# A two-block model in one program: row scales behind the matmuls, norms from PSUM per token tile, and the first loads on the weights' queue

## The chip, the cores and the metric

The kernel runs on one core of a Trainium2 chip. The metric is the time of one execution on the device in microseconds; the table below gives three runs. Everything is float32. TensorE (PE) multiplies, VectorE (DVE) and ScalarE (ACT) work on tiles of 128 partitions, GpSimd (POOL) and SyncE (SP) mostly issue DMAs.

## The reference, cut to what matters

The input x has 256 tokens of width 1024. A first block of two layers runs over it; each layer is FFN, mixer, FFN, with a norm ahead of and behind each:

```python
def rms_norm(x, g):
    return x * rsqrt(mean(x * x) + 1e-6) * g

for l in range(2):
    h = (silu(n(x, pre1) @ w_gate) * (n(x, pre1) @ w_up)) @ w_down      # width 2816
    x = x + 0.5 * rms_norm(h, post1)
    z = rms_norm(x, mix_pre) @ w_in                                     # 2840 columns
    # attention of three kinds on 1304 columns (with rope), a short convolution on the rest
    h = concat(rms_norm(attn, g_o), rms_norm(conv, g_u)) @ w_out
    x = x + rms_norm(h, mix_post)
    h = (silu(n(x, pre2) @ w_gate) * (n(x, pre2) @ w_up)) @ w_down
    x = x + 0.5 * rms_norm(h, post2)
```

A second block follows: modulation vectors, norms of a context and of x, a projection with a convolution and a state-space scan, a Fourier branch, a sum back into x, a norm, a router, 32 experts of which each token takes four, and a last norm.

## The kernel before, in words

All 256 tokens are worked on at once, as two token tiles of 128 (`m` = 0, 1). The weights come from memory in the order of use as chunks of 128 x 4096 floats (2 MB): SP loads them into a ring of three slots (`sp_stream`, L317). Products of the first block are made of three fp32r matmuls (`matmul3`, L376: hi x hi, hi x lo, lo x hi), so every chunk is cut into two halves, and each half is split: ACT writes the rounded part (`act_split`, L335), DVE the rest (`dve_split`, L347). There are two buffers for split halves. ACT may write one once PE is done with the half two before it. PE takes halves in order: `pe_wide` (L381) multiplies all k-tiles of a 512-column chunk for both token tiles, `pe_deep` (L398) the 1024-column chunks of a down-projection, k-tile by k-tile, with all four PSUM banks open. In both, PE writes banks 0 to 3.

Every engine has its own program, written out by hand in the order of `build` (L2133): each method `pe_...`, `act_...`, `dve_...`, `pool_...` appends to one engine, and semaphores (`up` and `at`) tie them together. An engine works strictly in that order. Two halves of the next stage's weights are always split ahead, so the last two splits of a stage's ACT and DVE programs belong to the next stage, and they stand ahead of the norm that ends the stage.

A norm ahead of a stage (`act_rstd` L419, `dve_rstd` L430): ACT squares both tiles with an accumulator, DVE scales and takes the reciprocal, ACT the square root. Then DVE scales tile 0 and ACT tile 1 by it into `xs` (L438, L444), PE transposes `xs` (`pe_turn`, L452), ACT writes the hi part with the gain as a column scale (L466), DVE the lo part (L480), and PE starts when all of it is there. The norm behind a stage (`act_add_normed` L498, `dve_add_normed` L507): ACT and DVE copy the four banks to `hout`, ACT squares, the root follows as above, and DVE, tile by tile, scales, multiplies by the gain row and adds to x. The same `rstd` helpers serve the merged norm in the mixer (L932, L934), the norms of the context and x, of y, of h2 and of the end in the second block.

In an FFN (L544 to L631) the gate and up chunks of one index `i` follow each other, Silu and product are made by ACT (L594) and DVE (L625), and the hidden part is transposed and split again. PE's gate of `i` waits for the Silu of `i-1`, which stands behind four splits on ACT.

At the start (`begin`, L2117) POOL issues the loads of constants, x, column constants, positions and the gain row, while SP already streams weights. DVE and ACT then make the rope tables, and only then split the first two halves.

Of the kernel before, what the change touches and what calls it, by code (L numbers as in the profile page):

```python
# [60 lines left out]
    "router_act": "top_exp WT",  # L61
}.items() for name in names.split()}
# [174 lines left out]
class Kernel:  # L237
# [79 lines left out]
    def sp_stream(self):  # L317
        sp, at, up = self.nc.sync, self.s.at, self.s.up
        for ch in self.chunks:
            if ch.c >= RING:  # L320
                sp.wait_ge(*self.freed_at(ch.c - RING))
            sp.dma_start(self.ring[ch.slot][:, 0:ch.kt * ch.width], ch.src).then_inc(*up(f"dma_ring{ch.slot}", ch.c))
# [12 lines left out]
    def act_split(self, n=1):  # L335

        act, at, up = self.nc.scalar, self.s.at, self.s.up
        for half in self.halves[self.act_half:self.act_half + n]:
            if half.j == 0:
                act.wait_ge(*at(f"dma_ring{half.chunk.slot}", half.chunk.c))  # L340
# [40 lines left out]
    def pe_wide(self, actT, banks, freed):  # L381
# [16 lines left out]
    def pe_deep(self, actT, kt, part_ready):  # L398
# [3 lines left out]
        while k0 < kt:  # L402
            half, w = self.pe_take()
            for k in range(half.k):
                if part_ready(k0 + k):
                    pe.wait_ge(*at(*part_ready(k0 + k)))
                for m in range(MT):
                    for h in range(2):
                        mm = self.matmul3(self.bank[2 * m + h][:, :], actT,
                                          (slice(None), k0 + k, slice(m * P, (m + 1) * P)),  # L410
                                          w, (slice(None), k, slice(h * 512, (h + 1) * 512)),
                                          k0 + k == 0, k0 + k == kt - 1)
            k0 += half.k
            mm.then_inc(*up("half_used", half.h))
# [15 lines left out]
    def dve_rstd(self, st, width, col):  # L430
        dve, at, up = self.nc.vector, self.s.at, self.s.up
        s = self.stat[:, col:col + MT]
        dve.wait_ge(*at("sum_sq", st, MT - 1))
        dve.tensor_scalar(s, s, 1.0 / width, EPS, ALU.mult, ALU.add).then_inc(*up("mean_sq", st))
        dve.wait_ge(*at("mean_sq", st))
        dve.reciprocal(s, s).then_inc(*up("inv_ms", st))
# [61 lines left out]
    def act_add_normed(self, st, done):  # L498
        act, at, up = self.nc.scalar, self.s.at, self.s.up
        act.wait_ge(*at(*done))  # L500
        for m in range(MT):
            act.copy(self.hout[:, m, 512:D], self.bank[2 * m + 1][:, :]).then_inc(*up("hout_right", st, m))
        act.wait_ge(*at("hout_left", st, MT - 1))
        act.wait_ge(*at("hout_right", st, MT - 1))
        self.act_rstd((st, "post"), self.hout, D, 0)

    def dve_add_normed(self, st, done, scale):  # L507
        dve, at, up = self.nc.vector, self.s.at, self.s.up
        h, s = self.hout, self.stat
        dve.wait_ge(*at(*done))  # L510
        for m in range(MT):
            dve.tensor_copy(h[:, m, 0:512], self.bank[2 * m][:, :]).then_inc(*up("hout_left", st, m))
        self.dve_rstd((st, "post"), D, 0)
        dve.wait_ge(*at("rstd", (st, "post")))
        dve.wait_ge(*at("dma_row", st))
        for m in range(MT):
            dve.tensor_scalar(h[:, m, :], h[:, m, :], s[:, m:m + 1], scale, ALU.mult,
                              ALU.mult).then_inc(*up("hout_scaled", st, m))
            dve.wait_ge(*at("hout_scaled", st, m))
            dve.tensor_tensor(h[:, m, :], h[:, m, :], self.row[:, :], ALU.mult).then_inc(*up("hout_gained", st, m))  # L520
            dve.wait_ge(*at("hout_gained", st, m))
            dve.tensor_tensor(self.x[:, m, :], self.x[:, m, :], h[:, m, :], ALU.add).then_inc(*up("x_new", st, m))
# [3 lines left out]
    def ffn_views(self):  # L526
        self.squares = view(self.work, 0, D)
        self.xs = view(self.work, 1024, MT, D)
# [10 lines left out]
    def pool_ffn(self, st, before, post_row):  # L539
        if before:  # L540
            self.nc.gpsimd.wait_ge(*self.s.at("x_new", before, MT - 1))
        self.nc.gpsimd.dma_start(self.row[:, :], post_row.partition_broadcast(P)).then_inc(*self.s.up("dma_row", st))

    def pe_ffn(self, st):  # L544
        pe, at, up = self.nc.tensor, self.s.at, self.s.up
        self.pe_turn(st, self.xs, KD, [("scaled0", st), ("scaled1", st)])
        pe.wait_ge(*at("turn_lo", st, KD // 2 - 1))
# [14 lines left out]
        for i in range(N_GU):  # L562
            self.gate_done[i] = self.pe_wide(self.xT, (0, 1), [i and ("silu", st, i - 1, m) for m in range(MT)])
# [7 lines left out]
        self.down_done = self.pe_deep(self.hT, KF, lambda k: None if k % 2 else ("hT_lo", st, k // 2))  # L571

    def act_ffn(self, st):
        act, at, up = self.nc.scalar, self.s.at, self.s.up
        act.wait_ge(*(at("x_new", self.before, MT - 1) if self.before else at("rope", 1)))
        self.act_rstd(st, self.x, D, 0)
        self.act_scaled(st, self.x, self.xs, 0)
        self.act_turn_hi(st, self.gain, self.xT, KD)
# [8 lines left out]
        for i in range(N_GU + 1):  # L587
# [3 lines left out]
            if i >= 2:  # L591
                act.wait_ge(*at("hid", st, i - 2, MT - 1))
# [1727 lines left out]
```

## Time and profile before

| | us |
|---|---|
| median of 3 runs | 3448.82 (3445.02 to 3450.51) |
| the profiled execution, its own time | 3445.97 |
| its span, first to last instruction | 3444.0 |
| PE busy | 2841.7 (83% of the span) |
| DVE busy | 1172.0 (34%) |
| ACT busy | 893.1 (26%) |
| POOL busy | 21.6 (1%) |
| DMA, mean over the span | 200 GB/s |

The first block takes the first 1450 us or so of the span, the second block up to the experts the next 1030, the experts the rest. The granted clock of PE is a share of 2.4 GHz; its mean over the span was 0.877.

### The profile page before, as it was taken

The numbers are of one execution on the slowest core, as the hardware profiler recorded it, in microseconds if no ns is written. First come the engines' busy times: TensorE is split into PE (matmuls) and PEld (weight loads), VectorE is DVE, ScalarE is ACT, GpSimd is POOL, SyncE is SP. The second block draws the span as 40 slices with busy tenths as digits, with TensorE's granted clock in tenths as the row PEclk, the third lists the DMA queues.
The fourth block names the chain that finished last, engine by engine and source line by source line (L and its number), as shares of the span: only waits on it lengthen the run. The fifth ranks groups of instructions, "written<-read, shape, count | busy, mean of one in ns | idle before, by whom it ended". The sixth has DMA issues, their size and how long they took to land.

```text
span 3444.0 us, 30326 instructions
## 1 busy us (share of the span) xinstructions
PE 2841.7 (83%) x12410; PEld 1787.5 (52%) x12410; DVE 1172.0 (34%) x1720; ACT 893.1 (26%) x1251; POOL 21.6 (1%) x48
## 2 busy tenths in 40 slices
PE   5987648979977579797976765888799999999997
PEld 4766447767764457613544444675544444444443
DVE  3444343444443444403444444544311111111112
ACT  3433233333333233303220110352111111111111
POOL 0000000000000000000000000000000000000000
PEclk9998669989987589998975765899699999999999
DMA  4443213434443034472110010342499999999999
GB/s 173 173 167 141 86 52 125 150 138 171 152 158 134 0 113 178 145 263 75 53 73 0 0 49 0 122 163 89 164 414 428 429 428 428 428 429 429 428 428 413
DMA packets 50420, 688.03 MB, mean 200 GB/s; under 512 B 5776, under 2 KB 5776, under 8 KB 8830
## 3 DMA queue, kind: packets, MB, share of 16 engines
q1 hardware_dynamic: 46800, 673.67, 48.9%
q0 software_dynamic: 3536, 13.16, 1.1%
q8 instruction: 62, 1.02, 0.1%
q14 instruction: 22, 0.18, 0.0%
HBM read 683.67 MB, written 1.05 MB: 199 GB/s over the span
## 4 chain that ended last, share of the span: by engine, by line
PE 80%; DVE 10%; ACT 7%; issue 2%; DMA 1%; POOL 0%; DVEq 0%; ACTq 0%; POOLq 0%
PE bank L378 32%; PE bank L1967 20%; PE bank L1283 6%; PE bank L1914 3%; PE bank L1159 2%; PE bank L1981 2%; PE bank L1957 2%; PE bank L1485 2%; ACT split_r L344 2%; PE bank L1479 1%; PE bank L1421 1%; ACT work L424 1%; PE bank L856 1%; PE bank L781 1%; PE bank L1470 1%
## 5 line engine op out<-in xcount | busy, mean ns | idle before, releaser
L378 PE MATMUL bank<-split_r,xT_r 128*128 128x512 f32 (+1 forms) x3456 | 806.0, 395 | 68.8 <-ACT work L594 43.3
L378 PEld LDWEIGHTS bank<-split_r,xT_r 128*128 128x128 f32 x3456 | 657.6, 193 | 213.2 <-issue 56.4
L353 DVE TENSOR_TENSOR split_r<-ring,split_r 128x2048 fp32r<-128x2048 f32 (+1 forms) x200 | 454.2, 2273 | 713.0 <-ACT split_r L344 713.0
L344 ACT CAST split_r<-ring 128x2048 fp32r<-128x2048 f32 (+1 forms) x200 | 378.2, 1893 | 769.2 <-PE bank L378 749.4
L1967 PE MATMUL bank<-ring,work 128*64 128x512 f32 x1536 | 344.8, 598 | 1.4 <-DVE work L1931 1.4
L378 PE MATMUL bank<-split_r,work_r 128*128 128x512 f32 x1344 | 315.8, 397 | 0.0
L378 PEld LDWEIGHTS bank<-split_r,work_r 128*128 128x128 f32 x1344 | 256.0, 191 | 57.5
L1967 PE MATMUL bank<-split,work 128*64 128x512 f32 x1024 | 232.2, 595 | 0.0
L1967 PEld LDWEIGHTS bank<-ring,work 128*64 128x64 f32 x1536 | 108.1, 138 | 230.0 <-issue 230.0
L1283 PE MATMUL bank<-work,ring 128*128 128x512 f32 (+1 forms) x512 | 203.5, 553 | 3.2 <-DVE work L1553 2.1
L462 PE MATMUL bank<-consts,work 128*128 128x128 f32 x176 | 38.8, 414 | 189.5 <-ACT work L441 178.3
L2017 DVE TENSOR_SCALAR work<-bank 128x512 f32<-128x512 f32 x32 | 22.2, 693 | 428.3 <-PE bank L1981 428.3
L1283 PEld LDWEIGHTS bank<-work,ring 128*128 128x128 f32 x512 | 99.0, 197 | 92.9 <-issue 84.8
L1967 PEld LDWEIGHTS bank<-split,work 128*64 128x64 f32 x1024 | 70.7, 137 | 130.1 <-issue 127.9
L1485 PE MATMUL bank<-work 128*128 128x64 f32 x256 | 59.1, 407 | 92.9 <-DVE work L1538 92.9
L462 PEld LDWEIGHTS bank<-consts,work 128*128 128x128 f32 x176 | 35.4, 223 | 192.6 <-DVE work L447 144.7
L1914 PE MATMUL bank<-work 128*128 128x64 f32 x1056 | 125.0, 278 | 0.0
L1914 PEld LDWEIGHTS bank<-work 128*128 128x128 f32 x1056 | 123.8, 196 | 1.5 <-issue 1.5
L1967 PE MATMUL bank<-work 128*64 128x512 f32 x512 | 115.3, 592 | 0.0
L1485 PEld LDWEIGHTS bank<-work 128*128 128x128 f32 x256 | 53.2, 308 | 101.3 <-DVE work L1538 101.3
L2019 DVE TENSOR_SCALAR work<-bank 128x512 f32<-128x512 f32 x32 | 22.2, 693 | 234.5 <-PE bank L1981 234.5
L1159 PE MATMUL bank<-ring,work 128*2 128x512 f32 x192 | 84.3, 602 | 18.9 <-ACT work L1145 18.9
(304 smaller groups left out, 2239.8 us busy)
## 6 DMA issues: line engine op xcount, KB each, us to landing
ring<-in_stream SPq DMA_DIRECT2D x219, 2048.0 KB, 8.7
split<-in_stream SPq DMA_DIRECT2D x66, 2048.0 KB, 15.4
work<-in_stream SPq DMA_DIRECT2D x33, 2048.0 KB, 14.0
ring<-in_stream SPq DMA_DIRECT2D x4, 1024.0 KB, 5.2
row<-in_rows POOLq DMA_DIRECT2D x6, 512.0 KB, 4.1
ring<-in_stream SPq DMA_DIRECT2D x2, 1120.0 KB, 7.4
work<-in_conv POOLq DMA_DIRECT2D x2, 768.0 KB, 5.7
x<-in_x POOLq DMA_DIRECT2D x1, 1024.0 KB, 19.4
```

Of the source, the lines that this page charges most:

```text
L344: act.copy(hi, self.part(half)).then_inc(*up("half_hi", half.h))
L353: dve.tensor_tensor(lo, self.part(half), hi.bitcast(F32), ALU.subtract).then_inc(*(self.freed_up(half.chunk.c) if half.ends_chunk else up( ...
L378: mm = self.nc.tensor.matmul(out, a[x][a_at], w[y][w_at], start=start and n == 0, stop=stop and n == 2)
L424: act.activation(self.squares[:, 0:width], src[:, m, :], ACT.Square, accum_out=self.stat[:, col + m:col + m + 1]).then_inc(*up("sum_sq", s ...
L462: tr = pe.transpose(self.bank[b][:, k * SEQ + m * P:k * SEQ + (m + 1) * P], src[:, m, (2 * q + k) * P:(2 * q + k + 1) * P], self.ident)
L1159: mm = pe.matmul(bank[c % 4][0:2, :], self.cs[:, k, :], w[:, k, :], start=(k == 0), stop=(k == KD - 1))
L1283: mm = pe.matmul(bank[n % 2][:, 0:(2 - s0) * SEQ], w[:, k, j * P:(j + 1) * P], self.h12[:, k, s0 * SEQ:2 * SEQ], start=(k == 0), stop=(k = ...
L1485: mm = pe.matmul(bank[6][:, (4 * half + hh) * HD2:(4 * half + hh + 1) * HD2], self.decay[half][:, hh, :], self.xdt[:, 4 * half + hh, :], s ...
L1914: mm = pe.matmul(bank[k // 4][:, k * SLOTS:(k + 1) * SLOTS], self.xs[:, m, k * P:(k + 1) * P], self.Pm[:, m, :], start=(m == 0), stop=(m = ...
L1957: mm = self.nc.tensor.matmul(self.bank[4 + 2 * m + h][:, :], self.PT[rows, m * P:(m + 1) * P], self.yb[rows, :], start=False, stop=stop)
L1967: mm = self.nc.tensor.matmul(self.bank[bank][h * SLOTS:(h + 1) * SLOTS, :], lhsT(k0 + k), w[:, k, h * 512:(h + 1) * 512], start=start and ...
L1981: mm = pe.matmul(bank[part][h * SLOTS:(h + 1) * SLOTS, :], self.sel[0:N_EXP, :], self.bias[0:N_EXP, part * D + h * 512:part * D + (h + 1) ...
```

## The change

- `act_rstd` squares with a scale, so that the accumulator holds the mean. The root moves from DVE and ACT to POOL (`pool_rstd`): an add of epsilon and a power of -0.5.
- The norm of x ahead of a stage of the first block is no longer applied to x. PE transposes x itself, quarter by quarter as it becomes ready (`pe_turn_x`), ACT and DVE make hi and lo parts of 128 columns (`act_turn_x`, `dve_turn_x`), and the row scale is applied behind the matmuls: as the scale of Silu, in DVE's hidden product, and in the z copies of the mixer. The squares of x are made by ACT behind its second split.
- The norm behind a stage works from PSUM, one token tile after the other: the last half of `pe_deep` runs tile 0 first, ACT squares its two banks, POOL makes the root, DVE multiplies bank and gain row, then scales and adds to x in one operation.
- Only one half is split ahead of a stage; the second is split between the left and the right lo parts on DVE, and behind all hi parts on ACT.
- x, column constants and constants are loaded first on SP's queue, the first chunk in two DMAs; positions stay on POOL. The rope tables are made by DVE behind the first turn of x, and by ACT behind `i` = 1 of the first FFN.

```diff
-def pe_wide(self, actT, banks, freed):
+def pe_wide(self, actT, banks, freed, turned=None):
...
+                if turned:
+                    pe.wait_ge(*at("turn_lo", turned, m, k0 // 4))
...
     def act_rstd(self, st, src, width, col):
...
-            act.activation(self.squares[:, 0:width], src[:, m, :], ACT.Square,
+            act.activation(self.squares[:, 0:width], src[:, m, :], ACT.Square, scale=width ** -0.5,
                            accum_out=self.stat[:, col + m:col + m + 1]).then_inc(*up("sum_sq", st, m))
-        act.wait_ge(*at("inv_ms", st))
-        act.activation(s, s, ACT.Sqrt).then_inc(*up("rstd", st))
...
+    def pool_rstd(self, st, col):
+        pool.wait_ge(*at("sum_sq", st, MT - 1))
+        pool.tensor_scalar(s, s, EPS, None, ALU.add).then_inc(*up("mean_sq", st))
+        pool.wait_ge(*at("mean_sq", st))
+        pool.tensor_tensor(s, s, self.stat[:, 62:62 + MT], ALU.pow).then_inc(*up("rstd", st))
...
+    def pe_turn_x(self, st):
+        for m in range(MT):
+            for h in range(2):
+                pe.wait_ge(*at(*self.x_done(m, h)))
+                for k in range(4):
+                    tr = pe.transpose(self.bank[4 + 2 * m + h][:, k * P:(k + 1) * P],
+                                      self.x[:, m, (4 * h + k) * P:(4 * h + k + 1) * P], self.ident)
+                tr.then_inc(*up("turned", st, m, h))
+    def act_turn_x(self, st, gain):
+        for m in range(MT):
+            for h in range(2):
+                act.wait_ge(*at("turned", st, m, h))
+                for k in range(4):
+                    i = act.activation(self.xT[0][:, 4 * h + k, m * P:(m + 1) * P], ..., scale=gain[...])
+                i.then_inc(*up("turn_hi", st, m, h))
+        self.act_split(1)
+        self.act_rstd(st, self.x, D, 0)
+    def dve_turn_x(self, st, gain):
+        for h in range(2):
+            if h:
+                self.dve_split(1)
+            for m in range(MT):
+                dve.wait_ge(*at("turn_hi", st, m, h))
+                for k in range(4):
+                    i = dve.scalar_tensor_tensor(self.xT[1][to], ..., ALU.mult, ALU.subtract)
+                i.then_inc(*up("turn_lo", st, m, h))
...
+    def act_add_normed(self, st, done, scale):
+        for m in range(MT):
+            act.wait_ge(*(at("first_tile", st) if m == 0 else at(*done)))
+            for h in range(2):
+                act.activation(self.squares[:, 0:512], self.bank[2 * m + h][:, :], ACT.Square, scale=D ** -0.5 / scale,
+                               accum_out=self.stat[:, 8 + 2 * m + h:9 + 2 * m + h]).then_inc(*up("post_sq", st, m, h))
+    def pool_add_normed(self, st, scale):
+        for m in range(MT):
+            pool.wait_ge(*at("post_sq", st, m, 1))
+            pool.tensor_scalar(r, sq[:, 0:1], sq[:, 1:2], EPS / scale ** 2, ALU.add, ALU.add)
+            pool.tensor_tensor(r, r, self.stat[:, 62:63], ALU.pow).then_inc(*up("post_rstd", st, m))
+    def dve_add_normed(self, st):
+        for m in range(MT):
+            for h in range(2):
+                dve.wait_ge(*at("post_sq", st, m, h))
+                dve.tensor_tensor(self.hout[:, m, cols], self.bank[2 * m + h][:, :], self.row[:, cols], ALU.mult)
+            dve.wait_ge(*at("post_rstd", st, m))
+            for h in range(2):
+                dve.scalar_tensor_tensor(self.x[:, m, cols], self.hout[:, m, cols], self.stat[:, 12 + m:13 + m],
+                                         self.x[:, m, cols], ALU.mult, ALU.add).then_inc(*up("x_new", st, m, h))
...
+                act.activation(self.sig[i % 2][:, m, 0:width], self.bank[m][:, 0:width], ACT.Silu,
+                               scale=self.stat[:, m:m + 1]).then_inc(*up("silu", st, i, m))
...
+            if i == 1 and not self.before:
+                self.act_rope()
...
-        self.act_split(KF // 2 - self.unsplit)
+        self.act_split(KF // 2 - 1 - self.unsplit)
...
     def begin(self):
-        pool.dma_start(self.consts[:, :], t["consts1"]).then_inc(*up("dma_first"))
-        pool.dma_start(self.x[:, :, :], ...)
+        sp.dma_start(self.x[:, :, :], t["x"].rearrange("(m p) d -> p m d", p=P)).then_inc(*up("dma_first"))
+        sp.dma_start(self.cols[...], t["cols1"].rearrange("l p n -> p l n")).then_inc(*up("dma_first"))
+        sp.dma_start(self.consts[:, :], t["consts1"]).then_inc(*up("dma_first", 0))
+        pool.dma_start(pos_i, t["positions"]).then_inc(*up("dma_pos", 0))
...
-        self.sp_stream()
         self.begin()
+        self.sp_stream()
```

## Rows read from the trace of the kernel before

**Rows 1.** The chain that ended last, its share by engine.
```profile
PE 80%; DVE 10%; ACT 7%; issue 2%; DMA 1%; POOL 0%; DVEq 0%; ACTq 0%; POOLq 0%
```

**Rows 2.** PE's waits: who for whom, us in total, times, longest.
```profile
PE bank L462 <- ACT work L441: 178.3, 9, 36.2
```

**Rows 3.** Timeline at the merged norm and y's: start, us, engine, [idle before].
```profile
463.73 0.63 ACT L424 ACTIVATE work<-work 128x512 f32<-128x512 f32 x1 [11.45 <-DVE work L1070]
...
470.38 3.65 PE L462 MATMUL bank<-consts,work 128*128 128x128 f32 x16 [16.02 <-ACT work L441]
...
2299.71 6.23 PE L462 MATMUL bank<-consts,work 128*128 128x128 f32 x32 [10.54 <-ACT work L441]
```

**Rows 4.** Timeline of the passage from the first FFN to the mixer.
```profile
248.15 1.90 ACT L344 CAST split_r<-ring 128x2048 fp32r<-128x2048 f32 x1 [3.53 <-PE bank L378]
...
250.08 2.29 DVE L353 TENSOR_TENSOR split_r<-ring,split_r 128x2048 fp32r<-128x2048 f32 x1 [3.13 <-ACT split_r L344]
...
262.71 1.22 DVE L522 TENSOR_TENSOR x<-x,work 128x1024 f32<-128x1024 f32 x1
...
268.51 3.65 PE L462 MATMUL bank<-consts,work 128*128 128x128 f32 x16 [20.39 <-ACT work L441]
...
270.51 3.43 DVE L491 SCALAR_TENSOR_TENSOR xT_r<-bank,cols,xT_r 128x256 fp32r<-128x256 f32 x8 [2.54 <-ACT xT_r L476]
...
274.00 26.25 PE L378 MATMUL bank<-split_r,xT_r 128*128 128x512 f32 x116 [1.84 <-DVE xT_r L491]
...
286.83 1.91 ACT L344 CAST split_r<-ring 128x2048 fp32r<-128x2048 f32 x1 [3.48 <-PE bank L378]
```

**Rows 5.** DMA in the first 80 us, 2 us a slice.
```profile
GB/s 82 213 410 439 403 442 422 430 430 432 354 224 0 0 0 0 0 131 369 401 147 0 0 0 0 0 0 0 8 57 221 442 320 8 0 164 360 442 82 0
```

**Rows 6.** Groups by line and shape: busy us, mean ns, idle before.
```profile
L424 ACT ACTIVATE work<-work 128x512 f32<-128x512 f32 x8 | 5.0, 625 | 24.7 <-DVE work L1070 24.6
...
L625 DVE TENSOR_TENSOR work<-work,bank 128x512 f32<-128x512 f32 x40 | 25.6, 680 | 0.0
...
L476 ACT ACTIVATE xT_r<-bank,cols 128x256 fp32r<-128x256 f32 x64 | 26.7, 470 | 10.5 <-PE bank L462 10.2
...
L1690 ACT CAST work_r<-bank 128x256 fp32r<-128x256 f32 x8 | 3.0, 374 | 4.7 <-PE bank L1650 4.7
...
L584 ACT CAST work_r<-bank 128x512 fp32r<-128x512 f32 x44 | 23.9, 601 | 10.3 <-PE bank L558 10.3
```

**Rows 7.** The same of POOL.
```profile
L742 POOL MEMSET work<- 128x512 f32 x2 | 1.1, 532 | 0.0
...
L1140 POOL MEMSET work<- 128x4 f32 x1 | 0.1, 123 | 0.0
```

**Rows 8.** A stretch: engines' busy time (count), granted clock, DMA share, GB/s.
```profile
274.00:280.00 6.00, 6.00 (x19) 4.86 (x20) 0.00 (x0) 0.00 (x0) 0.00 (x0) 0.71 0.00 0
```

**Rows 9.** Timeline of the start and the first FFN.
```profile
23.41 0.17 DVE L651 CAST stat<-work 128x2 f32<-128x2 int32 x1 [23.41 <-DMA work<-in_positions]
...
27.15 0.17 DVE L677 TENSOR_SCALAR work<-work 128x16 f32<-128x16 f32 x1
...
41.73 23.73 PE L378 MATMUL bank<-split_r,xT_r 128*128 128x512 f32 x96 [1.84 <-DVE xT_r L491]
...
69.44 23.56 PE L378 MATMUL bank<-split_r,xT_r 128*128 128x512 f32 x96 [3.99 <-ACT work L594]
...
95.58 22.05 PE L378 MATMUL bank<-split_r,xT_r 128*128 128x512 f32 x96 [1.71 <-ACT work L594]
```

**Rows 10.** Timeline of the passage into the second block.
```profile
1460.03 1.23 DVE L522 TENSOR_TENSOR x<-x,work 128x1024 f32<-128x1024 f32 x1
...
1468.48 4.08 PE L1159 MATMUL bank<-ring,work 128*2 128x512 f32 x5 [18.92 <-ACT work L1145]
```

**Rows 11.** Groups of table loads on ACT.
```profile
L428 ACT ACT_TABLE_LOAD x10 | 12.8, 1283 | 0.2
...
L594 ACT ACT_TABLE_LOAD x4 | 5.1, 1283 | 0.1
```

More of the change, by code:

```diff
@@ L403, in pe_deep @@
             half, w = self.pe_take()
[L404 to L412, printed above, removed]
+            whole = k0 + half.k < kt or first is None
+            for m0 in range(1 if whole else MT):
+                for k in range(half.k):
+                    if part_ready(k0 + k) and m0 == 0:
+                        pe.wait_ge(*at(*part_ready(k0 + k)))
+                    for m in (range(MT) if whole else (m0,)):
+                        for h in range(2):
+                            mm = self.matmul3(self.bank[2 * m + h][:, :], actT,
+                                              (slice(None), k0 + k, slice(m * P, (m + 1) * P)),
+                                              w, (slice(None), k, slice(h * 512, (h + 1) * 512)),
+                                              k0 + k == 0, k0 + k == kt - 1)
+                if not whole and m0 == 0:
+                    mm.then_inc(*up("first_tile", first))
             k0 += half.k
@@ L515, in dve_add_normed @@
+    def dve_add_normed(self, st):
+        dve, at, up = self.nc.vector, self.s.at, self.s.up
         dve.wait_ge(*at("dma_row", st))
         for m in range(MT):
[L517 to L521, printed above, removed]
@@ L570, in pe_ffn @@
         hidden_turned(i, FF_TAIL)
[L571 removed]
+        self.down_done = self.pe_deep(self.hT, KF, lambda k: None if k % 2 else ("hT_lo", st, k // 2), st)
     def act_ffn(self, st):
         act, at, up = self.nc.scalar, self.s.at, self.s.up
[L575 to L578, printed above, removed]
+        if not self.before:
+            self.act_split(1)
+        self.act_turn_x(st, self.gain)
         def hidden_hi(i, width):
@@ L641, in ffn, with rope_angles, act_rope, dve_rope @@
         self.dve_ffn(st)
-    def rope_tables(self):
-        dve, act, at, up, last = self.nc.vector, self.nc.scalar, self.s.at, self.s.up, self.s.last
-        pos_i = view(self.work, 0, MT).bitcast(I32)
-        w = view(self.work, 16, 6, MT, ROPE_HALF)
+    def rope_angles(self):
+        return view(self.work, WORK - 240, 6, MT, ROPE_HALF)
+    def act_rope(self):
+        for which in range(2):
+            self.nc.scalar.wait_ge(*self.s.at("angle", which))
+            self.nc.scalar.activation(self.rope[:, which, :, :], self.rope_angles()[:, 2 + 2 * which, :, :],
+                                      ACT.Sin).then_inc(*self.s.up("rope", which))
+    def dve_rope(self):
+        dve, at, up, last = self.nc.vector, self.s.at, self.s.up, self.s.last
+        pos_i = view(self.work, WORK - 256, MT).bitcast(I32)
+        w = self.rope_angles()
         pos = self.stat[:, 32:32 + MT]
-        dve.wait_ge(*at("dma_first", 0))
+        dve.wait_ge(*at("dma_pos", 0))
         dve.tensor_copy(pos, pos_i).then_inc(*up("angle"))
@@ L677, in rope_tables @@
             dve.tensor_scalar(r, r, -3.1415925, None, ALU.max).then_inc(*up("angle", which))
-            act.wait_ge(*at("angle", which))
-            act.activation(self.rope[:, which, :, :], r, ACT.Sin).then_inc(*up("rope", which))
     def dve_rotate(self, dst, src, m, nh, tmp, key):
```

167 lines of the change are left out of this document (88 added, 79 removed).

## The prediction

> **What bounds the kernel now.** I read the chain that ended last first: TensorE (PE) carries four fifths of it, VectorE (DVE) and ScalarE (ACT) most of the rest [rows 1]. So the question is where PE stands still. The waits view answers it: in front of the transposes of `pe_turn` PE waited 178.3 us in nine places, and the longest was 36.2 us, the start [rows 2]. Two of the nine are the merged norm inside the mixer (16.0 us each, one shown), and one, of 10.5 us, stands ahead of y's transposes [rows 3]; 178.3 - 36.2 - 32.0 - 10.5 = 99.6 us is left for the five passages from one stage of the first block to the next, 19.9 us each. The timeline of one passage shows what fills that time [rows 4]. Let T be the end of the last matmul of a stage, here 248.13. ACT splits one more weight half (T to T+1.9), DVE subtracts it (to T+4.2), both copy PSUM out, square, take the root, DVE scales, gains and adds (x is complete at T+15.8), ACT squares again, scales (T+20.2), PE transposes, and the next matmul starts at 274.00, T+25.9. The second half of the next stage's weights is used up at 286.83 (there ACT may refill its buffer), T+38.7. I compare on that mark, since the pipeline of halves runs as before behind it.
>
> The weights are no bound here: SP moves 2 MB per 48 matmuls of 0.23 us (11 us), and the DMA reached 430 to 440 GB/s [rows 5], 4.8 us for the same bytes.
>
> **A passage, worked anew (five times).** Removed from the path: the copies, the split of half N1 ahead of the norm, the row norm of x, a Sqrt table load, and two thirds of the vector work over 1024 columns. Durations: a Square over 512 columns with its accumulator 0.75 us (0.63 and 0.19, overlapping); a DVE operation over 512 columns with PSUM 0.68 alone, 0.64 in a row [rows 6]; one over 1024 SBUF columns 1.22 [rows 4], so 0.65 for 512. An ACT operation with a column scale takes 0.470 for 256 columns, without one 0.374, and a 512-column one 0.60 [rows 6]: 0.23 more for 256 columns, thus some 0.11 less for 128: 0.36 alone, 0.32 in a row. DVE's PSUM form goes at 3.43/8 = 0.43 for 256 [rows 4], less 128 columns at about 1 ns each: 0.30.
> GpSimd (POOL) never computes in this trace. Its add and pow on 128x1 or 128x2 are bounded by its memsets, 0.12 for 4 columns and 0.53 for 512 [rows 7]: a pair of the first is 0.3 us with the handovers, a pair of the second 1.2. Since pow is no memset I carry 3 us as outer end. My value is p = 0.8 us a pair, the middle of the two rows.
> - The last half of the stage runs tile by tile: first tile done at T-2.8. N0 was split before that, DVE free at T-1.2 (5.4 us ahead of N1's subtract, which ended at T+4.2 [rows 4]).
> - ACT squares tile 0 from T-2.7 to T-1.3, tile 1 from T to T+1.5. POOL: T-0.5, and T+2.3.
> - DVE: two multiplies T-1.2 to T+0.1, two scale-and-adds to T+1.4, two multiplies to T+2.7, two scale-and-adds to T+4.0. x is complete at T+4.0 instead of T+15.8. POOL stays under DVE's work up to p = 1.2.
> - PE's transposes (0.23 each) follow each quarter of x: first T+0.8, last T+5.1. ACT's 16 hi parts: T+1.9 to T+7.1; then split N1 to T+9.0, then the squares of x to T+11.4. On POOL the row norm waits for them, and in the mixer its memsets and shift DMAs stand behind it; these came 80 us into the mixer before: hidden.
> - DVE's lo parts: (tile 0, left) T+5.2, (1, left) T+7.0, split N1 T+9.0 to T+11.3, (0, right) T+12.5, (1, right) T+13.7.
> - PE: N0 from T+5.3 to T+10.8, a wait for the right part, N1 from T+12.5 to T+18.05.
> The saving is 38.7 - 18.05 = 20.6. The clock: behind the 20 us pause the granted clock was 0.71 in the first 6 us, that is partly 1.2 instead of 2.4 GHz [rows 8]. Behind a standstill of 4.0 us 96 matmuls took 23.56, behind one of 1.7 22.05 [rows 9]. In the new passage PE pauses in pieces of 1 to 2 us around its transposes. I cannot read from the trace whether this keeps 2.4 GHz, so I charge 1.0, between 0 and about 3 (mostly hidden by the wait at T+10.8). 19.7 a passage, 98.5 for five.
>
> **The start.** Before, positions lay last of the small loads beside the 6 MB stream: DVE's first work came at 23.41, the rope ended at 27.32, first matmul 41.73, first gate and up done at 65.46 [rows 9]. Now x, cols and consts (1.75 MB) are ahead of the stream. DMA moved 0.6 MB in the first 4 us and then some 0.42 MB/us [rows 5]: these are in at 7 to 8.5 us, the half chunk behind them (2.8 MB) at about 11 with a landing delay of one to two. ACT splits N0 to 12.9, DVE to 15.2; first left lo 16.4; PE N0 to 24 (cold); N1, behind its split (22.3) and the right lo part (23.5), 24 to 29.5. The stream is 4 us later by the loads put ahead of it, but its second chunk (7 MB in all, at 19) is wanted at 24 only. DVE then does the rope (3.9 us, 24.7 to 28.6; all splits of i=0 are queued behind its wait for the positions, which came at 23.4 before and now have no load but the stream beside them) and can split N2 only to 30.9, a loss of 1.4 behind N1. N2 and N3: 41.9. Gain 65.5 - 41.9 = 23.6. If positions land 5 us later than I allow, 3 us are gone.
>
> **Into the second block.** x was complete at 1461.26, T+11.7 as no split stood in the way, and PE started at 1468.48 [rows 10]. Now DVE starts at T-2.0 and ends at T+3.6; POOL's three DMAs and their landing move along: 8.1.
>
> **Table loads.** Each is 1.28 us; 10 stand at Sqrt, 4 at the Silu of the FFNs [rows 11]. Sqrt goes, so the third FFN needs no Silu load: its standstill shrinks from 4.0 by 1.28 and the clock stays (1.5): 2.8. The first and those behind a mixer (Exp) keep theirs. Sin moves into the first FFN behind i=1, where ACT idles 3.5 us ahead of each split [rows 4], but Silu is loaded again at i=2 on the path: 2.8 lost. If ACT's load were outside the path it would cost nothing.
> The Trainium skill, "ScalarE: Activation LUTs", section "What ACT_TABLE_LOAD costs", puts a drain of about 1.38 us on top of each load; by it both figures would grow by 1.4 and still cancel. Here the 3.99 us of the standstill at 69.44 are split 1.90, load 1.28, Silu 0.60 and handovers [rows 4, 6, 9, 11]; no drain fits in, so 1.28 stands.
>
> **Scales.** Silu with a column scale is 0.1 longer (0.470 - 0.374 [rows 6]); PE waits for tile 0's Silu at five places in four FFNs: 20 x 0.1 = 2.0 lost. The scale on z copies and on DVE's hid product is under matmuls of 11 us: 0; if it showed it would be under 0.1 each.
>
> **Other norms.** Merged, twice: from the first square at 463.73 to the transposes at 470.38 [rows 3]. Anew: two squares 1.5, p, scale and two squares 2.1, p, scale 0.7, handover 0.15 = 4.5 + 2p = 6.1, against 6.65: 0.6 each, 1.2. With p = 3 it would be 3.8 slower. ctx, y and end lose a load and a root (1.5) for 0.8: 0.7 each; x1 and h2, without a load, lose 0.2 each. 1.7.
>
> **Sum.** 23.6 + 98.5 + 8.1 + 2.8 - 2.8 - 2.0 + 1.2 + 1.7 = 131 us. The profiled execution took 3445.97 (span 3444.0), 3 below the median 3448.82; 3446 - 131 = 3315.
>
> **Rivals.**
> - *The new passage is only two thirds filled.* One of: the instructions over 128 columns cost as those over 256 (0.43 for both; ACT +1.7, then N1's split and all behind it), the clock falls in each passage (+2 more), p = 2 (+0.8). For: hi and lo now are 32 instructions instead of 16 and stand in series with N1's split. Against: the slope per column [rows 6]. Some 4.5 a passage less, and 3 at the start: 3315 + 5 x 4.5 + 3 = 3341.
> - *The passage does better*: full clock (-1 each), p = 0.4, positions early, and ACT's first conv Silu also without its load: 3305.
> - *GpSimd becomes the bound, and the kernel is slower.* POOL does tile 0's pair and then tile 1's; once p is above some 2 us, x is complete at about T+1.3+2p. Path slope: 2 for each of six passages, 2 for each of two merged norms, 1 for five norms: 21 us per us of p. The 131 us are gone at p = 0.8 + 131/21 = 7 us; p = 10 gives 3508. For: no POOL arithmetic is in the trace, and POOL works in order, so that tile 1's pair waits for tile 0's. Against: its rows of 0.12 to 0.53 us, and that a pair on two columns has nothing to stream. The Trainium skill, "GPSIMD Engine Reference", section "Instruction dispatch", states about 6 us for the first call to freshly loaded code: paid once it would be under 3322 in all, paid at each pair it would just reach the point of this rival; no run here shows it.
> - *The gain was hidden anyway*, PE runs into the weights: 3440. Against it 4.8 us of DMA a chunk under 11 us of PE [rows 5].
>
> The Trainium skill, "SBUF — State Buffer", section "SBUF: two separate sides", says that a GpSimd operation and a DVE operation with two SBUF inputs block each other for a whole instruction. Here this would hold POOL's pair for tile 1 behind one scale-and-add (0.65 at most), and the same DVE operations behind it: up to 0.7 a passage, 3319 in all. No row of the trace before can show it.
>
> **Numbers.** Forecast 64% (3300 to 3330), two-thirds rival 25%, better 8%, GpSimd 2%, hidden 1%. Range 3294 to 3346: below it a passage shorter by 4 us than worked out, above it p = 3 (3361) and the slower rival, with the hidden gain. Under 0.2% (7 us) this measurement can't tell from no change: faster 0.96, same 0.01, slower 0.03.
>
> **What would show it.** PE's pause between stages: first transposes under 1 us behind the last matmul, first matmul at about T+5.3, N1 used at T+18 to T+20. x complete at T+4. POOL's add and pow together under 1 us. First matmul at 16 to 18 us. One standstill of 4 us at i=2 of the first FFN, none in the third. The granted clock between T and T+10. Wrong would be: a pair on POOL over 2 us, hi parts above 0.4 us, PE waiting for positions, or new waits for the ring.

## The result, and the profile after

The changed kernel took 3319.47 us (median of 4 executions, 3317.41 to 3326.43), the kernel before 3449.66 in the same series (3445.02 to 3454.08): a ratio of 0.963, with a 95% interval of 0.9618 to 0.9642. That is 130 us less; 131 were forecast, and 3315 us. The profiled execution took 3317.65 us with a span of 3315.8, before 3445.97 and 3444.0, so the two traces differ by 128.2 us of span.

The first question to a pair of traces is whether TensorE (PE) works less or stands less. Part 1 of the page of the changed kernel gives each engine's busy time, part 4 the chain's shares:

```profile
PE 2837.7 (86%) x12410; PEld 1781.9 (54%) x12410; DVE 1153.7 (35%) x1720; ACT 872.8 (26%) x1271; POOL 45.1 (1%) x99
...
PE 82%; DVE 8%; ACT 5%; issue 3%; DMA 1%; POOL 0%; SPq 0%; DVEq 0%; ACTq 0%; POOLq 0%
```

PE was busy for 2841.7 us before and for 2837.7 now, with the same 12410 matmuls. So 4.0 of the 128.2 us are matmuls that ran at a higher clock (mean granted clock 0.877 before, 0.889 now), and 124.2 are standstill that is gone. Its share of the chain rose from 80% [rows 1] to 82%. The waits of PE, where [rows 2] had one entry of 178.3 us in nine places:

```profile
PE bank L383 <- ACT work L658: 43.7, 20, 4.1
PE bank L472 <- ACT work L451: 42.3, 3, 16.1
PE bank L620 <- DVE work L693: 16.9, 4, 4.2
PE bank L518 <- DVE x L583: 10.1, 10, 1.4
```

L472 are the transposes that stayed as they were: the two merged norms and y's. The five passages are now L518 (the transposes of x straight from x), ten waits of about 1 us. The largest entry of the first block is the wait of a gate's first matmul for ScalarE's Silu; it is an old one (43.3 us before).

One passage, from the first FFN to the mixer, answers to [rows 4]. T, the end of the last matmul, is 225.72 (226.46 less the 0.74 in its brackets):

```profile
222.25 2.29 DVE L358 TENSOR_TENSOR split_r<-ring,split_r 128x2048 fp32r<-128x2048 f32 x1 [3.20 <-ACT split_r L349]
223.01 0.60 ACT L558 ACTIVATE work<-bank 128x512 f32<-128x512 f32 x1 [0.79 <-PE bank L383]
...
224.46 1.28 DVE L577 TENSOR_TENSOR work<-bank,row 128x512 f32<-128x512 f32 x2
224.52 0.31 POOL L566 TENSOR_SCALAR stat<-stat 128x1 f32<-128x1 f32 x1 [200.12 <-ACT work L558]
224.91 0.57 POOL L568 TENSOR_TENSOR stat<-stat 128x1 f32<-128x1 f32 x1
225.66 1.40 DVE L583 SCALAR_TENSOR_TENSOR x<-work,stat,x 128x512 f32<-128x512 f32 x2
...
226.46 1.32 PE L518 MATMUL bank<-consts,x 128*128 128x128 f32 x8 [0.74 <-DVE x L583]
...
228.25 1.41 DVE L583 SCALAR_TENSOR_TENSOR x<-work,stat,x 128x512 f32<-128x512 f32 x2
229.06 1.32 PE L518 MATMUL bank<-consts,x 128*128 128x128 f32 x8 [1.28 <-DVE x L583]
...
230.85 15.45 PE L383 MATMUL bank<-split_r,xT_r 128*128 128x512 f32 x60 [0.47 <-DVE xT_r L544]
...
235.96 2.15 DVE L544 SCALAR_TENSOR_TENSOR xT_r<-bank,cols,xT_r 128x128 fp32r<-128x128 f32 x8
...
238.23 1.91 ACT L349 CAST split_r<-ring 128x2048 fp32r<-128x2048 f32 x1 [2.28 <-PE bank L383]
...
243.61 1.91 ACT L349 CAST split_r<-ring 128x2048 fp32r<-128x2048 f32 x1 [3.48 <-PE bank L383]
```

x is complete at 229.66, T+3.9 (T+15.8 before). The next stage's first matmul starts at T+5.1 (T+25.9 before). Its first half of weights is used up at 238.23, where ScalarE may refill the buffer, and the second at 243.61, T+17.9 (T+38.7 before). GpSimd's root of a tile is two instructions of 0.30 and 0.57 us and lies beside VectorE's products out of PSUM.

The start, against [rows 9]:

```profile
9.51 3.39 PE L518 MATMUL bank<-consts,x 128*128 128x128 f32 x16 [9.51 <-DMA consts<-in_consts]
11.93 1.28 ACT L349 ACT_TABLE_LOAD   x1 [11.93 <-DMA ring<-in_stream]
13.23 1.90 ACT L349 CAST split_r<-ring 128x2048 fp32r<-128x2048 f32 x1
...
18.71 23.98 PE L383 MATMUL bank<-split_r,xT_r 128*128 128x512 f32 x96 [5.81 <-DVE xT_r L544]
...
25.37 0.15 DVE L728 CAST stat<-work 128x2 f32<-128x2 int32 x1
...
46.76 0.77 PE L383 MATMUL bank<-split_r,xT_r 128*128 128x512 f32 x1 [4.08 <-ACT work L658]
```

### The profile page after: what moved, and what is told of

It is laid out like the page before. It is cut to its first block, busy times and chain, and to the rows that moved or that the text cites. A ratio compares the mean times of both kernels' runs of the same rounds, so it can differ in the third digit from the quotient of the medians.

```text
span 3315.8 us, 30424 instructions
## 1 busy us (share of the span) xinstructions
PE 2837.7 (86%) x12410; PEld 1781.9 (54%) x12410; DVE 1153.7 (35%) x1720; ACT 872.8 (26%) x1271; POOL 45.1 (1%) x99
## 4 chain that ended last, share of the span: by engine, by line
PE 82%; DVE 8%; ACT 5%; issue 3%; DMA 1%; POOL 0%; SPq 0%; DVEq 0%; ACTq 0%; POOLq 0%
PE bank L383 33%; PE bank L2042 20%; PE bank L1358 6%; PE bank L1989 4%; PE bank L1236 3%; PE bank L2056 2%; PE bank L2032 2%; PE bank L1560 2%; PE bank L1554 2%; PE bank L1496 1%; PE bank L934 1%; ACT split_r L349 1%; PE bank L859 1%; PE bank L1545 1%; DMA ring<-in_stream 1%
## 5 line engine op out<-in xcount | busy, mean ns | idle before, releaser
L383 PE MATMUL bank<-split_r,xT_r 128*128 128x512 f32 (+1 forms) x3456 | 804.2, 394 | 66.5 <-ACT work L658 43.7
L383 PEld LDWEIGHTS bank<-split_r,xT_r 128*128 128x128 f32 x3456 | 655.9, 192 | 210.0 <-issue 67.5
L383 PE MATMUL bank<-split_r,work_r 128*128 128x512 f32 x1344 | 317.6, 399 | 0.0
L383 PEld LDWEIGHTS bank<-split_r,work_r 128*128 128x128 f32 x1344 | 257.3, 192 | 58.1
L1236 PE MATMUL bank<-ring,work 128*2 128x512 f32 x192 | 83.8, 599 | 11.2 <-ACT work L1222 11.2
L1427 DVE SCALAR_TENSOR_TENSOR work<-work 128x512 f32<-128x512 f32 (+1 forms) x128 | 87.8, 686 | 4.5
L2081 ACT COPY work<-bank 128x256 f32<-128x256 f32 x32 | 12.0, 375 | 286.0 <-PE bank L2063 286.0
```

Source lines behind the costliest of these rows:

```text
L383: mm = self.nc.tensor.matmul(out, a[x][a_at], w[y][w_at], start=start and n == 0, stop=stop and n == 2)
L1236: mm = pe.matmul(bank[c % 4][0:2, :], self.cs[:, k, :], w[:, k, :], start=(k == 0), stop=(k == KD - 1))
L1427: dve.scalar_tensor_tensor(a, src, wt, a, ALU.mult, ALU.add).then_inc(*(up("tap", n) if tap == 4 else up("tap")))
```

## The experiments

Nine kernels ran beside the kernel before, each timed in 4 executions; the intervals of their ratios are about 0.002 wide to each side, some 7 us. Marks are moments of the profiled execution; T is again the end of the stage's last matmul, here the start of the row of the first transposes less the idle time in its brackets. The kernels ran in three series (the yardstick to the norm ahead of a stage; the next four; the last), in which the kernel before took 3450.85, 3449.02 and 3446.31 us. Differences in us across two series therefore carry 2 to 5 us more of doubt.

**The yardstick.** The changed kernel once more.

> The changed kernel with all of its work, the yardstick of the runs beside it (only the value that the last waits of its loops compare with is kept from going below zero). Both theories: 3319 us, within 0.2% of the changed kernel's 3319.47.

3319.84 us, ratio 0.9621 (0.9597 to 0.9646). All experiments below derive from it, and their line numbers differ by a few from the changed kernel's.

**The loads of x and the constants behind the stream again.**

```diff
-sp.dma_start(self.x[:, :, :], t["x"]...)      # cols and consts likewise, then sp_stream
+self.sp_stream()                               # now ahead of begin
+pool.dma_start(self.x[:, :, :], t["x"]...)     # cols and consts likewise
```

> x and the constants are loaded on GpSimd's queue behind its own set-up again and the weight stream starts first on SP's queue; all else is the changed kernel. Theory A (the order of the loads is most of what the start gains): x is ready for ScalarE's first split at about 26 us instead of 13.2, as the same loads were before the change, and the whole ends 12 to 14 us later, 3332 us. Rival B (the start gains from the norm's row scales and from RoPE's tables standing behind, and the loads are hidden beside the memsets and the first weights): at most 2 us, 3320.

3331.01 us (0.9652; 0.963 to 0.9675), 11.2 more. Theory A's mechanism holds, a little under its size of 12 to 14, and at three quarters of it in the trace: the first FFN's second gate starts at 56.09 instead of 46.69, 9.4 later.

```profile
5.93 1.28 ACT L352 ACT_TABLE_LOAD   x1 [5.93 <-DMA ring<-in_stream]
22.53 1.90 ACT L352 CAST split_r<-ring 128x2048 fp32r<-128x2048 f32 x1 [15.31 <-DMA consts<-in_consts]
```

x and the constants landed at 22.5 and not at 26 as I had expected, and ScalarE's table load now stood under the wait (5.93), where in the changed kernel it is on the path (11.93). The positions moved behind these loads too; nothing separates their share.

**GpSimd's power twice.**

```diff
+pool.tensor_tensor(self.stat[:, 56:56 + MT], s, self.stat[:, 62:62 + MT], ALU.pow)
+pool.wait_ge(*self.s.last("spare"))
 pool.tensor_tensor(s, s, self.stat[:, 62:62 + MT], ALU.pow)      # and so in each tile's pair
```

> GpSimd does the power of each pair twice (a spare result, waited for), which makes each pair about 0.75 us longer; all else is the changed kernel. Theory A (where the norm is one tile's, GpSimd's second pair lies on the path to x and to the next stage's first matmul; where it is merged, both pairs do): 0.75 us at each of the five passages and the entry into the second block, 1.5 at each of the two merged norms, 0.75 at each of about five other norms: +11, 3330 us. Rival B (GpSimd's root is hidden behind VectorE's products and ScalarE's squares, and at most the merged norms see it): +3 at most, 3322. Rival C (each longer standstill also lowers the granted clock): over +20.

3336.66 us (0.9668; 0.9648 to 0.9688), 16.8 more, between A's 11 and C's 20. The standstills say A: PE waits 17.63 us ahead of the merged norm's transposes where the yardstick waits 16.09 (two powers of 0.77 with their handover), and in a passage VectorE now waits for GpSimd before both tiles (0.38 and 0.27 us), which it did not before:

```profile
891.30 1.41 DVE L590 SCALAR_TENSOR_TENSOR x<-work,stat,x 128x512 f32<-128x512 f32 x2 [0.38 <-POOL stat L575]
...
894.18 1.41 DVE L590 SCALAR_TENSOR_TENSOR x<-work,stat,x 128x512 f32<-128x512 f32 x2 [0.27 <-POOL stat L575]
```

The size does not come from there alone: of 19.1 us between the two spans, PE's busy time is 10.1 (2851.1 against 2841.0, at a mean granted clock of 0.884 against 0.890), and 9.0 are standstill. That the longer pauses caused the lower clock (a weak form of C) is not settled by this; the mean clock of one kernel's executions scatters too (0.884 to 0.887 here, 0.886 to 0.890 in the yardstick).

**The norm ahead of a stage as before.**

```diff
-act.activation(self.sig..., ACT.Silu, scale=self.stat[:, m:m + 1])   # no row scales behind matmuls
+act.activation(self.sig..., ACT.Silu)
-self.pe_turn_x / act_turn_x / dve_turn_x: transposes of x, hi and lo per quarter
+act_rstd, GpSimd's root, x scaled into xs, pe_turn, turn_hi, turn_lo over both tiles
```

> The norm ahead of a stage as it was before the change (root, the whole x scaled into another tensor, then turned; no row scales behind the matmuls), while the norm behind a stage, the start's loads and the splits stay as changed. Theory A (the passage gains this half because squares, root and scaling of x leave the path to the first matmul): first stage matmuls about 9 us later at each of five passages and 8 at the entry into the second block, 5 at the start, less 2 that the Silus with a row scale cost: +50 to +56, 3372 us. Rival B (most of it was hidden behind the transposes or is given by the norm behind the stage): +20 at most, 3340.

3369.56 us (0.976; 0.9737 to 0.9782), 49.7 more: A. In the passage behind the first mixer T is 474.26:

```profile
478.24 1.06 ACT L438 ACTIVATE work<-x 128x1024 f32<-128x1024 f32 x1 [0.75 <-DVE x L600]
...
481.74 1.15 ACT L452 ACTIVATE work<-x,stat 128x1024 f32<-128x1024 f32 x1 [1.17 <-POOL stat L447]
...
483.03 3.65 PE L473 MATMUL bank<-consts,work 128*128 128x128 f32 x16 [8.77 <-ACT work L452]
...
488.51 18.84 PE L386 MATMUL bank<-split_r,xT_r 128*128 128x512 f32 x69 [1.84 <-DVE xT_r L502]
```

Squares, root, scaling and the undivided transposes stand in series and the first matmul comes at T+14.3 instead of T+5.1. At the start this half is worth 9.95 us (second gate at 56.64 instead of 46.69), twice what I had written. Part of it is not the norm: the edit also puts ScalarE's second split, 1.9 us, ahead of the squares, and at the start that split is on the path (in the passages the squares wait for x, the 0.75 above). The scales show here too: without them PE waits 41.8 us for the Silus instead of 43.7, and 16.4 instead of 16.9 ahead of the last transposes of `hid`.

**The norm behind a stage as before.**

```diff
-act Square out of PSUM per half; dve h = PSUM * row; dve x = h * r + x
+act and dve copy PSUM to hout; act Square of hout; root
+dve h = h * r * scale; dve h = h * row; dve x = x + h      # tile after tile
```

> The norm behind a stage as it was before the change (both halves copied out of PSUM, squares of the copy, root, scale, gain and addition as three operations on VectorE, tile after tile), while the norm ahead of a stage, the loads and the splits stay as changed. Theory A (this half is worth the time from the end of the last matmul to the complete x, 11.4 us with the copies and 3.9 without): +7.5 at each of five passages and the entry into the second block, about +1.5 at the merged norms and +3 at others: +45 to +50, 3367 us. Rival B (only the halves that the first transposes want matter, since the other tile's work runs beside them): +20, 3340.

3362.62 us (0.9759; 0.9737 to 0.9781), 42.8 more: A, a little under its size. T is 468.61 in this one:

```profile
468.66 1.29 DVE L591 COPY work<-bank 128x512 f32<-128x512 f32 x2 [1.15 <-PE bank L386]
...
476.22 1.97 PE L521 MATMUL bank<-consts,x 128*128 128x128 f32 x8 [7.61 <-DVE x L602]
```

The first transposes come at T+7.6 instead of T+0.8, in each passage: PE waits for x ten times and 44.4 us in all, where the changed kernel has 10.1; into the second block it waits 18.6 us instead of 11.2.

**Two halves split ahead of each stage again.**

```diff
-self.act_split(1)              # act_turn_x, dve_turn_x: the second half, behind the hi parts
-self.act_split(1); self.dve_split(1)          # act_ffn, dve_ffn, ahead of the first FFN
+self.act_split(2); self.dve_split(2)
-self.act_split(KF // 2 - 1 - self.unsplit)    # a stage's last splits, one less;
+self.act_split(KF // 2 - self.unsplit)        # dve_ffn and the mixer's end likewise
```

> The engines split both halves of two chunk pairs ahead of each stage again, where the change splits one; all else is the changed kernel. Theory A (the fewer splits between the stages lie on the path, each 128 by 1024 split of about 1.8 us standing ahead of the squares or the low parts): +2 to +4 at each of five passages, +10 to +20, 3335 us. Rival B (those splits fill time in which the engines wait for the last matmuls): within 2 us of 3319.

3342.85 us (0.9692; 0.9675 to 0.9708), 23.0 more: A's mechanism, a little above its size of 10 to 20. The edit for which the prediction had no term of its own is worth a sixth of the whole. T is 466.10:

```profile
466.14 1.90 ACT L352 CAST split_r<-ring 128x2048 fp32r<-128x2048 f32 x1 [3.48 <-PE bank L386]
467.94 0.59 ACT L558 ACTIVATE work<-bank 128x512 f32<-128x512 f32 x1
468.07 2.29 DVE L361 TENSOR_TENSOR split_r<-ring,split_r 128x2048 fp32r<-128x2048 f32 x1 [3.08 <-ACT split_r L352]
...
469.44 1.09 POOL L566 TENSOR_SCALAR stat<-stat 128x1 f32<-128x1 f32 x1 [34.59 <-ACT work L558]
...
471.66 0.98 POOL L568 TENSOR_TENSOR stat<-stat 128x1 f32<-128x1 f32 x1
...
472.27 1.97 PE L521 MATMUL bank<-consts,x 128*128 128x128 f32 x8 [6.17 <-DVE x L583]
```

ScalarE's last split stands ahead of its first square, which starts at T+1.8 instead of T-2.7, and VectorE's subtraction stands ahead of the products. PE waits 33.6 us for x, where the yardstick has 10.1.

**A better place for the Silus.** The changed kernel's largest wait in the first block, 43.7 us, is ScalarE's own order: four splits, then two Silus, while the Silus' input was ready two splits earlier.

```diff
-self.act_split(4 if i < N_GU else 2)
+self.act_split(2)
 ... two Silus ...
+if i < N_GU:
+    self.act_split(2)
```

> In the FFN ScalarE does its Silus after two of its four splits instead of behind all four; all else is the changed kernel. Theory A (the wait of the next gate's first matmul for the Silu, 1.8 us twenty times, is ScalarE's place for the Silus in its own order, and the splits are not urgent): about 1.6 us gone in each of the sixteen full iterations and some 4 in each first one: -40 to -47, 3275 us. Rival B (the splits are what the matmuls wait for in truth, and the wait moves to the split weights): no gain or slower, 3319 or above. Rival C: the pause goes, but the clock that the pauses let the engine keep falls instead: a gain under 20.

3261.51 us (0.9454; 0.9437 to 0.947), 58.3 less than the yardstick, and more than A had. The entry L383 <- L658 of the waits is gone. The gate of the second chunk pair in the second FFN, where the yardstick waits 4.08 us, follows the first pair without a pause (55 matmuls in one row, which begins with the window; both Silus and their table load beside them):

```profile
463.66 12.63 PE L386 MATMUL bank<-split_r,xT_r 128*128 128x512 f32 x55
465.11 1.28 ACT L661 ACT_TABLE_LOAD   x1
...
466.40 1.27 ACT L661 ACTIVATE work<-bank,stat 128x512 f32<-128x512 f32 x2
```

Between the two spans lie 53.6 us: 43.7 of waits, and 10.5 of PE's busy time (2830.5 against 2841.0), since more of the matmuls behind the removed pauses run at the higher clock. C is the wrong way round.

**The same in the narrow iteration.** One split, Silu, one split on ScalarE; one split, the product, one split on VectorE.

```diff
-self.dve_split(4 if i < N_GU else 2)
+self.dve_split(4 if i < N_GU else 1)
 ... hid ...
+if i == N_GU:
+    self.dve_split(1)
```

> As the kernel with the Silus between the splits, and in the last narrow iteration ScalarE and VectorE do their Silu and product after one split each, so that the down projection's pause of 4.2 us in each of the four FFNs shrinks to 1 or 2. Theory A: -10 to -17 against the kernel with the Silus between the splits, 3262 us. Rival B (the down projection's first matmuls want the splits that are now later): no gain, 3275.

3239.22 us (0.9393; 0.9377 to 0.9409), 22.3 less than the one before it. The wait ahead of the last transposes of `hid` falls from 4.23 us to 0.70, four times, that is 14.1, within A's range by itself; PE's busy time falls by another 14.5 (2816.0), and the gain comes out above it. The 14.5 compares two single executions, though, and the one profiled before it was the slowest of its four (3266.01 against a median of 3261.51); the medians leave some 8 us beside the waits.

```profile
568.62 0.66 PE L623 MATMUL bank<-consts,work 128*128 128x128 f32 x4 [0.70 <-DVE work L697]
```

**The convolution inside the attention.** The merged norm's wait, 16.1 us twice, is the one that the change left alone.

```diff
 for i, (b, m, g) in enumerate(self.units):
+    if i == 3: conv_taps()       # six products, were behind the loop
+    if i == 5: conv_sum()        # two sums and a product, were behind the loop
     ...                          # u's squares at i == 5, its scaling at i == 6
-self.dve_scaled((st, "u"), ...)  # after o's, behind the loop
```

> As the kernel with the narrow iteration's Silus between the splits; in the mixer VectorE does the short convolution (six products, two sums, a product, 7.4 us) in its idle time inside the attention instead of behind it, and u's squares, root and scaling are done there too, so that behind the attention only o's norm is left. Theory A (PE's wait of 16.1 us ahead of the merged norm's transposes is VectorE's convolution and then two norms in series with GpSimd's pair in each): the wait shrinks to about 5.5 us, -10.6 in each of two mixers: 3239 - 21 = 3218 us. Rival B (VectorE or ScalarE is what the attention's matmuls wait for, and the work inserted there is paid there): 3232 or above. Rival C (the clock falls less or more behind the shorter wait): within 3 us of A.

3216.77 us (0.933; 0.9311 to 0.9348), 22.4 less than the one before it, where A had 21. The wait is 5.34 us. C's time is the same as A's, so the time does not tell them apart; PE's busy time did not move (2816.9):

```profile
395.76 0.63 ACT L440 ACTIVATE work<-work 128x512 f32<-128x512 f32 x1 [5.68 <-DVE work L1164]
...
399.17 1.08 PE L475 MATMUL bank<-consts,work 128*128 128x128 f32 x4 [5.34 <-DVE work L460]
```

This kernel beats both: 103 us under the changed one (100 by the ratios of the two series), 230 under the one before.

## Why the prediction was right, step by step

The four undone parts cost 11.2, 49.7, 42.8 and 23.0 us, 127 in all, against the 130 that they bring together. As far as four intervals of some 7 us each can tell, they hardly overlap, and not much is outside them; the root on GpSimd was not undone by itself. So the forecast was right for its reasons in the two large terms, and its passages are where the time came from. Several small terms failed, and that their errors cancelled to within 2 us is luck. By its terms:

- **The passage.** Forecast: x complete T+4.0, first matmul T+5.3, N1 used T+18.05. Measured: T+3.9, T+5.1, T+17.9. The last of the three agrees in part by luck. N0 was to be used up at T+10.8, and PE was to wait for the right lo part until T+12.5. In fact hi and lo parts of 128 columns are shorter than the slopes gave (0.27 us each for a hi part where 0.32 was taken, 0.27 to 0.28 for a lo part where 0.30 was), and the first right lo part was there at T+11.4. But the granted clock was 0.67 in N0's first 5.2 us (below), N0 lasted until T+12.3 (ScalarE's refill follows at 238.23), and N1 followed without a wait. The fourth passage (T is 882.23) had the full clock: N0 takes 5.69 us, PE waits 0.70 for the lo part, and N1 is used up at T+17.2:

```profile
887.34 5.69 PE L383 MATMUL bank<-split_r,xT_r 128*128 128x512 f32 x24 [0.47 <-DVE xT_r L544]
893.73 22.77 PE L383 MATMUL bank<-split_r,xT_r 128*128 128x512 f32 x120 [0.70 <-DVE xT_r L544]
```

  So the lower clock costs up to 0.7 us in a passage, under the 1.0 charged. It came in four passages of five, in the yardstick too, but there the second had the full clock and the fourth not: part of it is chance. From T to N1's mark the passages gave 20.8, 20.8, 21.0, 21.5 and 19.8 us, 104 in all, where 20.6 each was worked out ahead of the charge. Between wider marks, which leave nothing out, the two traces draw apart by 20.9, 18.9, 21.9, 20.1 and 17.2 us, 99.0; with the third FFN's table load (1.3) taken out and the dearer Silus (about 1.4) put back this is 99.1 against 98.5. That the mean is 19.8, as with the 1.0 that I charged, comes from matmuls between the passages that met the lower clock in one trace and not in the other, and not from where the charge was put. The rival "two thirds" had its chance mostly from the durations for 128 columns and from 2 us of clock a passage.
- **The start.** 23.6 forecast, 22.7 measured (second gate 69.44 [rows 9] to 46.76). The first matmul came at 18.71 and not at 16.4: the half landed at 11.9 instead of 11, and ScalarE then loaded a table for 1.28 us, which no step had. It cost little, because VectorE's rope work (25.37 to 29.27, against 24.7 to 28.6) is what N2 and N3 wait for.
- **Into the second block.** PE's start moved from T+18.9 to T+11.2 (DMA latency and a Silu are left): 7.75 against 8.1.
- **Scales.** 1.80 instead of 1.71 us at each standstill, 20 times: 1.8 against 2.0. The scale on z costs nothing that shows. Ahead of the last transposes of `hid` it does show, against the forecast: PE waits 4.24 us there instead of 4.11, in four FFNs, 0.5 in all (16.9 against 16.4; the undone scales gave 16.4 again).
- **Table loads.** Both terms failed, and their errors partly cancelled. Sin did not force a reload: in the first FFN there is no load between the Silus, the two rope instructions at L719 and the next Silus. So the -2.8 was 0:

```profile
44.63 1.28 ACT L658 ACT_TABLE_LOAD   x1
...
72.21 1.26 ACT L658 ACTIVATE work<-bank,stat 128x512 f32<-128x512 f32 x2
...
74.30 0.35 ACT L719 ACTIVATE rope<-work 128x16 f32<-128x16 f32 x2
```

  The third FFN's standstill did shrink by the load, from 4.0 to 2.67, but the 96 matmuls behind it took 23.56 us, as they did before behind 4.0 [rows 9]: the 1.5 for the clock did not come, and the term was 1.3. That "the clock stays" for a shorter pause was read from 1.71 us. Behind 2.67 us the runs went both ways: with the loads put back the same 96 matmuls took 22.05, in the yardstick and with the doubled power 23.6.

```profile
230.80:236.00 5.20, 5.15 (x16) 4.12 (x17) 3.38 (x6) 5.12 (x10) 0.33 (x1) 0.67 0.79 252
...
702.20:708.00 5.80, 5.80 (x19) 4.66 (x20) 2.89 (x3) 0.41 (x1) 0.00 (x0) 0.72 0.57 171
```

(The first row is the first passage, the second the third FFN behind its pause. Stretch, its length, busy time and count of PE, PEld, DVE, ACT and POOL, granted clock, DMA share, GB/s.)

- **GpSimd's pair and the other norms.** This term was mis-sized, by its whole 2.9 us. p = 0.8 was the middle of two memset rows; the groups of GpSimd by shape show

```profile
L446 POOL TENSOR_TENSOR stat<-stat 128x2 f32<-128x2 f32 x15 | 10.8, 720 | 1.3
L568 POOL TENSOR_TENSOR stat<-stat 128x1 f32<-128x1 f32 x12 | 6.7, 562 | 1.0
L566 POOL TENSOR_SCALAR stat<-stat 128x1 f32<-128x1 f32 x12 | 3.6, 303 | 869.3 <-ACT work L558 869.3
L444 POOL TENSOR_SCALAR stat<-stat 128x2 f32<-128x2 f32 x15 | 3.4, 226 | 1766.1 <-ACT work L437 1766.1
```

  0.95 us a pair on two columns (0.87 on one) and with the handovers 1.17 from the last square to the scaled tile (423.52 to 424.69). In the passages that is under VectorE's products, as foreseen up to 1.2. In the merged norm nothing covers it: 6.65 us from the first square to the transposes [rows 3] became 6.71, where 6.1 was forecast, twice. ctx, x1, y and h2 changed by -0.1, +0.4, -0.4 and +0.6 us of PE's wait instead of -0.7, +0.2, -0.7 and +0.2. Together these norms brought nothing where 2.9 stood in the sum.
- **The rivals.** GpSimd as the bound is refuted by the pair's 0.95 us; the power doubled shows the slope that the rival used, in standstill 9 us for 0.77 us more, 12 per us and not 21, since a part stays under VectorE. The 6 us that the Trainium skill, "GPSIMD Engine Reference", section "Instruction dispatch", puts on the first call to freshly loaded code were not there: the program's first pair started at 23.37, 0.08 us behind ScalarE's last square, and took 0.22 and 0.72 us. Whether its code was freshly loaded no run shows. "Hidden anyway" fell with the passages. "Better" (3305) had a full clock and p = 0.4; neither came, the first in one passage only.

The sum by measured terms: 22.7 + 99.1 + 7.75 + 1.3 + 0 - 1.8 + 0 = 129 (start, passages, second block, third FFN, Sin, scales, other norms) against 128.2 between the spans.

## What to carry to other kernels

When a stage boundary is long because norms stand in series with transposes and splits, write the boundary anew on one time axis from the last matmul, engine by engine, and compare at one mark behind which the pipeline is unchanged: that gave x's completion, the first matmul and the last mark within 0.2 us here, though moments between them were off by up to 1.5 and cancelled, while terms "in passing" (a table load, a middle value between two unlike rows) were wrong by their whole size. Then look at the order of work inside the engines that feed the matmuls: moving two Silus ahead of two splits brought nearly half as much as this change, and moving the convolution's nine VectorE instructions and the norm of `u` into idle time a sixth.

## What the runs showed of the hardware

- **GpSimd waits for VectorE on SBUF.** A GpSimd add on one column takes 0.30 us. In the kernel with whole splits it took 1.09, from 469.44 to 470.53, while VectorE did a subtraction with both inputs in SBUF until 470.36, and it took 1.08 to 1.09 in all five passages; the power of the next tile took 0.98 instead of 0.57 beside VectorE's scale-and-add. Beside products with one input in PSUM (227.27, 227.65 in the changed kernel) the same two took 0.30 and 0.57. The Trainium skill, "SBUF — State Buffer", section "SBUF: two separate sides", says that a VectorE operation with two SBUF inputs and a GpSimd operation hold the shared port for a whole instruction. For GpSimd's side these rows agree; that VectorE is held up by GpSimd no run here shows. The change escapes it only because its pairs fall beside operations that read PSUM; the prediction's 0.7 a passage did not come.
- **A pause can cost more than its length.** Removing 43.7 us of pauses of 1.8 to 4.1 us brought 58.3 in the medians, and removing 14.1 brought 22.3. PE's busy time fell by 10.5 and 14.5 us: fewer matmuls met the lower clock. Removing 21.5 us in the two pauses of 16.1 brought 22.4, with PE's busy time unchanged. Behind a pause of 1.8 us alone the traces show both: 96 matmuls in 22.05 us at most places, 23.65 to 23.67 at two in the run with the doubled power, at two with the loads put back and at one in the yardstick. What decides between them stays open.
- **Silu and Sin need one table load here**, and the first ScalarE instruction of the program needs one too, 1.28 us, which costs nothing only if it comes before its data.
